# Grouped-key attention: who makes the reciprocals of the softmax sums

## What is computed

```python
def gqa_attend(q, k, v):
    s = jnp.einsum('bqhgd,bkhd->bhgqk', q, k).astype(jnp.float32) * (GQA_HEAD_DIM ** -0.5)
    p = jax.nn.softmax(s, axis=-1).astype(v.dtype)
    return jnp.einsum('bhgqk,bkhd->bqhgd', p, v)
...
    o = sweep_query_blocks(lambda qb: gqa_attend(qb, k_all, v_all), q).reshape(B, S, GQA_WIDTH)
    y = (o * jax.nn.silu(g)) @ p["w_out"]
```

## Time and profile before

| | |
|---|---|
| median of 3 runs | 3474.52 us |
| profiled execution | 3474.66 us |
| its span, first to last instruction | 3472.9 us |
| granted TensorE clock, mean | 0.989 of full speed |
| gqa phase | about 1810 to 2330 us of the span |
| mla phase | about 2840 to 3395 us of the span |

### The profile page before, as it was taken

The page is one execution under the profiler, slowest core; times in us unless marked ns, Lnnn a source line. Parts: engine busy times, 40 slices in busy tenths (PEclk is TensorE's granted clock), DMA queues, the critical chain, the costliest instruction groups (busy, mean ns, idle before and its releaser), DMA issues.

```text
span 3472.9 us, 48071 instructions
## 1 busy us (share of the span) xinstructions
PE 3345.5 (96%) x15063; PEld 2669.0 (77%) x15063; DVE 2256.5 (65%) x2664; ACT 1770.3 (51%) x3036; POOL 1516.2 (44%) x952
## 2 busy tenths in 40 slices
PE   7999999899999999999999999999998999999999
PEld 5777878778888888778877777778675668888877
DVE  6674878677576665748627777767548875555551
ACT  3342868432010100234329999981454658888880
POOL 3402444544444444310037777767220026666662
PEclk9999999999999999999999999999999999999999
DMA  2134232411212121122353444323245344332312
GB/s 102 49 115 129 61 83 55 152 49 56 90 47 93 50 80 65 40 85 106 122 132 81 86 106 91 75 75 121 100 176 168 127 132 113 69 79 60 79 36 80
DMA packets 196088, 313.56 MB, mean 90 GB/s; under 512 B 100928, under 2 KB 111680, under 8 KB 195968
## 3 DMA queue, kind: packets, MB, share of 16 engines
q1 hardware_dynamic: 195968, 312.01, 31.2%
HBM read 234.02 MB, written 77.92 MB: 90 GB/s over the span
## 4 chain that ended last, share of the span: by engine, by line
PE 68%; POOL 10%; issue 9%; DVE 8%; ACT 4%; DMA 0%; ACTq 0%; POOLq 0%; DVEq 0%; SPq 0%
PE PBX L281 11%; PE PBX L283 11%; PE PBX L282 11%; POOL gqa_pl L2232 9%; PE PMX L281 5%; PE PMX L282 5%; PE PMX L283 5%; PE PMX L2095 2%; PE PD L2140 2%; PE PD L924 2%; PE PD L2141 2%; PE PBX L2122 2%; PE PBX L2121 2%; PE PD L2142 2%; PE PBX L2123 2%
## 5 line engine op out<-in xcount | busy, mean ns | idle before, releaser
L216 POOL TENSOR_TENSOR w_hi<-w_stage,zero 128x1024 fp32r<-128x1024 f32 (+2 forms) x123 | 229.4, 1865 | 1253.0 <-PE PBX L283 762.5
L2232 POOL TENSOR_TENSOR gqa_pl<-gqa_pf,gqa_ph 128x512 fp32r<-128x512 f32 (+1 forms) x288 | 381.7, 1342 | 140.8 <-ACT gqa_ph L2188 139.4
L2232 POOL TENSOR_TENSOR mla_pl<-mla_pf,mla_ph 128x512 fp32r<-128x512 f32 x256 | 341.6, 1340 | 189.9 <-ACT mla_ph L2188 184.5
L218 POOL TENSOR_TENSOR w_lo<-w_stage,w_hi 128x1024 fp32r<-128x1024 f32 (+2 forms) x123 | 303.0, 2463 | 9.6
L2254 DVE TENSOR_REDUCE mla_m<-PMX 128x1 f32<-128x1280 f32 x126 | 187.9, 1492 | 172.8 <-PE PMX L2095 172.7
L2254 DVE TENSOR_REDUCE gqa_m<-PMX 128x1 f32<-128x1280 f32 (+1 forms) x142 | 198.6, 1398 | 155.0 <-PE PMX L2095 154.3
L1785 ACT ACTIVATE conv_in<-PBX 128x512 f32<-128x512 f32 x66 | 39.6, 601 | 480.3 <-PE PBX L283 476.6
L2182 ACT ACTIVATE mla_pf<-PBX 128x512 f32<-128x512 f32 x320 | 190.4, 595 | 74.9 <-PE PBX L2123 60.6
L2188 ACT ACTIVATE gqa_ph<-gqa_pf 128x512 fp32r<-128x512 f32 (+1 forms) x352 | 215.0, 611 | 12.4 <-PE PD L2142 0.4
L2182 ACT ACTIVATE gqa_pf<-PBX 128x512 f32<-128x512 f32 (+1 forms) x352 | 201.0, 571 | 30.4 <-PE PBX L2126 25.3
L281 PE MATMUL PBX<-ffn_hi,w_hi 128*128 128x512 f32 x528 | 206.8, 392 | 3.8 <-DVE ffn_lo L698 3.8
(11 more groups left out here) (510 smaller groups left out, 9956.4 us busy)
## 6 DMA issues: line engine op xcount, KB each, us to landing
mod_w<-in_w_mod SPq DMA_DIRECT2D x48, 512.0 KB, 3.5
w_stage<-in_w_up SPq DMA_DIRECT2D x44, 512.0 KB, 3.5
w_stage<-in_w_go SPq DMA_DIRECT2D x24, 512.0 KB, 3.6
gqa_k<-kh_d SPq DMA_DIRECT2D x32, 320.0 KB, 4.8
gqa_q<-qh_d SPq DMA_DIRECT2D x32, 320.0 KB, 6.9
w_stage<-in_w_down SPq DMA_DIRECT2D x24, 384.0 KB, 3.1
qh_d<-heads_qh SPq DMA_DIRECT2D x32, 256.0 KB, 2.1
ql_d<-heads_ql SPq DMA_DIRECT2D x32, 256.0 KB, 2.3
```

The costliest lines, as they stand in the source:

```text
L216: pool.tensor_tensor(w_hi[s][:, 0:st.cols], w_stage[s][:, 0:st.cols], z, ALU.add).then_inc(w_hi_done, 1)
L218: pool.tensor_tensor(w_lo[s][:, 0:st.cols], w_stage[s][:, 0:st.cols], w_hi[s][:, 0:st.cols].bitcast(F32), ALU.subtract).then_inc(w_split, 1)
L2232: eng.tensor_tensor(self.PL[k % 4][:, 0:n], self.PF[k % 4][:, 0:n], self.PH[k % 4][:, 0:n].bitcast(F32), ALU.subtract).then_inc(self.lo_dv ...
```

## The change

For gqa, ScalarE's queue no longer holds `rden`. VectorE's `final` waits for the chunk's value products itself, makes the reciprocal from PSUM into `gqa_rd` with one instruction, and goes on as before, at the same places of its queue. The mla attention is as it was.

```diff
                         def reciprocal():
-                            self.ended(rden, i, k, lags)
+                            if self.mla:
+                                self.ended(rden, i, k, lags)
...
                     h = slice(64 * q, 64 * q + 64)
-                    dve.wait_ge(self.rden, i * (4 * NC) + (2 * x + 2))
+                    if self.mla:
+                        dve.wait_ge(self.rden, i * (4 * NC) + (2 * x + 2))
+                    else:
+                        dve.wait_ge(self.pv, i * SB + (k + CR_PV2 + 1))
+                        dve.reciprocal(self.RD[:, 0:n], self.O[c][64:128, 0:n]).then_inc(self.rden, 1)
+                        dve.wait_ge(self.rden, i * (2 * NC) + (x + 1))
                     dve.wait_ge(self.fin, i * (2 * NC) + (x + CR_FIN2))
```

## The result

The changed kernel takes 3558.63 us (median of three runs, 3558.49 to 3561.63), the kernel before 3474.52. The ratio is 1.0246, with a 95% interval of 1.0232 to 1.0260: 84 us slower. The forecast was 3620 us, the range 3535 to 3700.

A forecast was written before the change was run, and what follows sets the result against it. The prediction took TensorE as the bound before and VectorE after the change: +120 us for VectorE's queue, +25 for the clock, nothing back for ScalarE, +145 on 3474.66 us, forecast 3620 us, range 3535 to 3700.

The forecast's parts named there:

- What bounds the kernel now: Gqa phase: TensorE sets the pace, ScalarE second by 5 us, VectorE with 14.5 us of room in a 64.0 us pair.
- Removed: ScalarE loses 6.5 us a pair at chunk ends; gain between nothing and 50 us over eight pairs.
- Added: VectorE's reciprocals at eight passes: 4.42 us for 512 columns, 2.28 us for 256, 22.2 us a pair.
- The sum in VectorE's queue: VectorE becomes the bound: 72.6 us of queue plus 6.4 us of waits, 79.0 us a pair, +120 us over eight pairs.
- The six-pass case: Low end of the main case: reciprocals 16.9 us a pair, no fall of the clock, +78 us, 3553 us.
- The signs: Expected in the trace: VectorE 90% or more busy, pair 79 to 83 us, TensorE waiting some 17 us for maxima.
- The holds: TensorE held at tiles of maxima, 3.6 us at the first and 4.8 us at the second chunk end of every head.
- One fall of the clock per head: TensorE's clock drops after a hold, costing 2.4 us of matmul time, some 1.6 us reaching VectorE's queue; 25 us.
- Two to five passes: Rival: cheaper reciprocals on VectorE, at four passes 11.5 us a pair, +34 us, 3509 us; chance 0.07.
- one pass: Rivals: VectorE's reciprocal costs a multiplication's 0.68 us; either faster, 3458 us, chance 0.07, or within 0.2% of 3474, chance 0.06.

The follow-up runs named there:

- holding the clock up: Changed kernel with 14 unused products in TensorE's queue ahead of each tile of the context chunk's maxima; 3548.98 us, ratio 1.0219.
- The run with a copy: Changed kernel with a copy of the sums from PSUM in place of each reciprocal, so the output is not divided; 3455.07 us, ratio 0.9950.
- the run with transposed sums: Changed kernel with sums transposed in 32x32 blocks, the reciprocal made of one column per block, then transposed back repeated; 3508.86 us, ratio 1.0103.
- the run with pieces: Changed kernel with each head's reciprocals cut into seven pieces spread over VectorE's steps and the multiplications moved later; 3536.45 us, ratio 1.0184.

## Why the prediction was right, and where it was off

*What bounds the kernel now.* Right: TensorE, with ScalarE near and VectorE with room.

*Removed.* The bounds of 0 and 50 us hold: 21 us alone, nothing beside the reciprocals, as the sum had it.

*Added.* The step that was mis-sized. I took eight passes, 4.42 and 2.28 us; the trace has 3.36 and 1.76, which is six, the lower end of the arithmetic that I gave: 17.0 us a pair in place of 22.2. The four shapes seen (16, 128, 256 and 512 columns: 0.25, 0.96, 1.76 and 3.36 us) fit 0.16 us and 6.25 ns per column. The Trainium skill ("VectorE: DVE Perf Modes", "First, the fixed hardware budget") gives a repeat count of 8; the order of size agrees, but 3.36 us lies under the estimate of 4.27 that follows from it, and the measurement decides. The Trainium skill's "Vector Engine (DVE) Microarchitecture Reference", section 3.2, read as one column each cycle, is excluded: 3.36 us is five times the 0.68 us of a multiplication.

*The sum in VectorE's queue.* I had 79.0 us a pair and 3.1 us for the clock, 82.1; the pair is 75.3. Its parts: reciprocals 5.2 us less, as said. VectorE's other work 4.8 us less (61.3 - 17.0 = 44.3 in place of 49.1), which I had kept fixed:

```profile
L2233 DVE TENSOR_TENSOR gqa_pl<-gqa_pf,gqa_ph 128x512 fp32r<-128x512 f32 x8 | 5.5, 686 | 0.1
L2284 DVE TENSOR_TENSOR MIX<-gqa_t,gqa_gate 64x512 f32 x4 | 4.9, 1224 | 0.7 <-DVE gqa_t L2279 0.2
...
L2263 DVE TENSOR_TENSOR gqa_d<-ident_f,gqa_m 128x512 fp32r<-128x512 f32 x4 | 2.8, 692 | 0.3
```

The diagonal took 1.25 us before and the low part up to 1.54; both are now at 0.69, while GpSimd waits 29.5 us a pair for copies. The multiplications into `MIX` went the other way, 1.3 us a pair more, with 1.76 us for the one behind the second chunk's reciprocal. That such instructions are slow while GpSimd runs is my reading. The timelines agree: GpSimd subtracts without a break from 1993.12 to 2000.33 us around the slow diagonal of the kernel before; in the changed one from 1992.71 to 2000.35 us, which takes in most of the slow `MIX`, and it stands idle when the fast diagonal follows at 2002.34. No run separates it. And the waits for maxima are 12.0 us where I had 6.4, plus 3.1 for the clock: 2.5 us too low. Starts and small gaps take another 0.7 us (2.0 us in place of 1.3), though a multiplication starts 0.03 us behind its reciprocal and not the 0.15 us that I took from another row. That is 82.1 - 5.2 - 4.8 + 2.5 + 0.7 = 75.3. Here the step itself was weak: VectorE is the bound only from a quiet step's end to the next reduction, and in the quiet steps TensorE, with its two steps between tiles, sets the pace as before. The bound changes hands twice per head, so most of the old waiting stays. The error of 61 us is (18.1 - 11.3) x 8 = 54 us from the pairs and the rest from the first and last heads.

*Luck.* The six-pass case in my range, 3553 us, comes within 6 us of the result, and that is partly luck: it leaves out the falls of the clock and has the waits too low and the other work too high, errors that go against each other.

*The signs.* VectorE was busy for 81% of the pair (61.3 of 75.3 us), where I had named 90% or more; TensorE waited 11.2 us a pair for maxima, where I had some 17; ScalarE's activations took 53.7 us for 52; the clock was at 0.95 and mla as before. At the end of the phase the last reciprocals cost 5 us, the few microseconds that I had put inside the roundings.

*The holds.* Forecast 3.6 us at the first chunk end and 4.8 at the second; measured 1.4 and 4.1 to 4.2. One fall of the clock per head was right in number; I gave it 25 us, and holding the clock up gave 8 to 10.

*The rivals.* Two to five passes and one pass are excluded by the row of the RECIPROCAL. The run with a copy shows that one pass would have gained 18 us, where I had set 17. That such a change would stay faster up to 1.2 us was not tried.

## What to carry to other kernels

Ask of an instruction that moves to an engine with room not whether its sum fits there, but what stands behind it in the queue and who waits for that: 53.8 us of the same instruction cost 16 us ahead of one tile and 50 us ahead of another. A wait that an engine shows in quiet stretches can't be spent at a busy one. And a reciprocal on VectorE costs six multiplications' worth per column here, so have it run over as few columns as the data allow: over 16 in place of 512 it took 0.25 us, 1.7 us with both transposes, in place of 3.36.

## What the runs showed of the hardware

RECIPROCAL on VectorE took 0.16 us and 6.25 ns per column for 64 rows of float32, for 128 to 512 columns from PSUM; 16 columns from SBUF took 0.25 us, which the same line gives; a copy of 64x512 from the same bank took 0.69 us and a transpose in 32x32 blocks 0.72 us, also where its source is one column repeated 32 times (0.70 us). The granted clock was 0.51 behind a hold of 4.1 us, and stayed at 1.00 behind holds of 1.4 us; with holds of 3.1 us, only the second chunk moved, the pair's mean was 0.95. The length of the one hold didn't settle it: the clock fell behind one of 1.67 us in the run with transposed sums, and behind one of 2.07 us but not behind one of 1.93 us in the run with pieces.
